# A two-block transformer on one core: copies, norms and gate tiles reordered around the weight splits, output in four pieces

## The chip, the cores and the metric

The kernel is one launch on one core of a Trainium2 chip. The metric is the device time of that launch in microseconds, from the chip's profiler. Engines are named PE (TensorE; PEld is its weight load), DVE (VectorE), ACT (ScalarE), POOL (GpSimd) and SP (SyncE, which issues DMAs). Each engine runs its own instructions in program order; between engines there are semaphores.

## The reference

All is fp32. The activations are x, 1 x 256 x 1024; two memories of 256 x 1024 are attended to. Cut to its shape:

```python
def first_block(x, mem, ...):                       # DEPTH = 2
    for layer in range(DEPTH):
        mix = even_mixer(x, ...) if layer % 2 == 0 else odd_mixer(x, ...)
        x = layer_norm(DEEPNORM_ALPHA * x + mix, ...)
        x = layer_norm(DEEPNORM_ALPHA * x + memory_cross_attention(x, mem, ...), ...)
        x = layer_norm(DEEPNORM_ALPHA * x + swiglu(x, ...), ...)

def second_block(x, mem, ...):
    for l in range(DEPTH):
        x = layer_norm_2(DN_ALPHA * x + 0.5 * swiglu_ffn(x, ffn_w_in[l, 0], ffn_w_out[l, 0]), ...)
        x = layer_norm_2(DN_ALPHA * x + mixer_sublayer(x, ...), ...)
        x = layer_norm_2(DN_ALPHA * x + memory_cross_attention_2(x, mem, ...), ...)
        x = layer_norm_2(DN_ALPHA * x + 0.5 * swiglu_ffn(x, ffn_w_in[l, 1], ffn_w_out[l, 1]), ...)
```

The even mixer is four heads of a two-directional mLSTM (a chunked scan with decays and a running maximum) beside eight heads of neighbourhood attention. The odd mixer is differential attention with rotary positions and an RMS norm per head. `mixer_sublayer` adds three branches, each behind a sigmoid gate and a projection: attention over a latent of width 128 restricted to the 64 best keys of each query, stick-breaking attention, and a short causal convolution.

## The kernel before

**Stages.** `SUB` lists 14 stages, j = 0 to 13: even, cross, ffn, odd, cross, ffn, then twice ffn, merge, cross, ffn. "Merge" is `mixer_sublayer`. A cross of the first block has four heads of 256 and is called long here; one of the second block has four heads of 128 and is called single. The whole program is written out instruction by instruction for each engine; there is no loop on the chip.

**Products and weights.** Every fp32 product is three matmuls (helper at L354): high part of the one by high part of the other, and the two mixed ones. So every operand is split into a high and a low half. A weight tile is 128 x 2048 elements, 1 MB. SyncE transfers it into a ring of RAW = 3 buffers, ScalarE copies the high half out (`wh`, L1226), VectorE subtracts to get the low half (`wl`, L1754). The raw buffer is free for another transfer when both have read it. The split tiles stand in a ring of PARTS = 3. The first tiles of a stage ("entry tiles") have places of their own, named front, side, back, mem, note and under. The activations of a stage are transposed by TensorE and copied out of PSUM as `xh` (ScalarE, L1257) and `xl` (VectorE); attention outputs likewise as `oh` and `ol` (L1788, L2201).

**What sets the order.** `get(name, look)` on ScalarE and VectorE is "wait for the PSUM bank `name`"; ahead of that wait it makes the split of every weight tile that TensorE will use up to `look` tiles beyond the bank's own (PARTS − 1 by default; None makes none, `ahead(name, look)` only splits). A copy or a norm written behind such a call therefore stands behind the split, 1.8 us on ScalarE and 2.2 us on VectorE. `take` hands TensorE its PSUM banks in turn, `free` gives one back when it has been copied, `await_read` waits for that.

**Even stage** (TensorE L772 on, ScalarE L1420 on, VectorE L1997 on). VectorE copies `av` (L2055) out of two banks after the wait for Silu and a scaling of the keys (L2050); the decay maxima follow (L2066), then on ScalarE the copies `cn` (L1482). In the neighbourhood attention TensorE per unit does scores, products of the output projection, head outputs, and the transpose of the probabilities.

**Cross stages.** `softmax` (ScalarE L1317 on, VectorE L1884 on) goes through the heads: maxima, exponentials, normalisation (L1916), and `after(t)`, the copies of head outputs. `out_proj` (L510 on) does the output projection in steps (half of x, four k parts); with kc = 4 (single cross) its first step may start with a part of the input ready ("gradual"). It also places the entry tiles of the next stage. VectorE then adds the residual (L1844), norms and stores x (L1868), one half of 512 columns after the other. In a single cross VectorE copies `xv` (L1937) and makes the low parts `ol` before it.

**Odd stage.** `enter` (L560 on) runs the first projections over the entry tiles. In the attention loop VectorE does maxima, a rotary step `rope(t + 2)` and the probabilities of the unit before (L2156 on).

**Merge.** The last loop (TensorE L1136 on) has steps t = −1 to 11. Step t does the transposes of unit t − 2, the scores of unit t, for odd t the next two query products (`ql`, copied by ScalarE L1710), the latent products of unit t − 3, and for t ≥ 0 half a gate tile (a gate is `x` by a 1024 x 256 slice, ScalarE makes the sigmoid `gs`, L1613). `LATENT_GATES` says at which step ScalarE reads a finished gate. Then come four column groups n of three branch products each, with the last four gate tiles between them, and `merged` parts (L2420 on).

**Output.** SyncE waits for the last x and stores all of it by one DMA (L2618 to L2620).

## Time and profile before

| | before |
|---|---|
| median of 3 runs | 2274.41 us (2272.13 to 2275.5) |
| the profiled execution | 2275.15 us |
| its span in the trace | 2273.4 us |
| PE busy | 2218.6 us, 98% |
| PEld busy | 2055.5 us, 90% |
| DVE busy | 1436.1 us, 63% |
| ACT busy | 1063.6 us, 47% |
| POOL busy | 103.5 us, 5% |
| mean DMA rate | 181 GB/s |

The time of an execution is that of the device, the span runs from the first to the last instruction in the trace; 1.75 us lie outside it. "Busy" counts the time in which an engine works on an instruction. PE at 98% leaves 54.8 us in which it does nothing. In the 40 slices of the page PE stands at 9 (90% or more) in all but the last, where it is 8, and so does PEclk, the clock that the throttle granted. By stages, from the timeline: even from 14 to 162 us, long crosses to 282 and at 576 to 705, odd 465 to 576, merges about 1080 to 1290 and 1781 to 1983, single crosses 1340 to 1396 and 2042 to 2088. The last matmul ends at 2263.9, the last x at 2268.9 us.

### The profile page before, as it was taken

The page shows a single profiled execution, that of the slowest core. Times are in us where ns is not written, and L with a number is a line of the kernel's source. Part 1 is how long each engine was busy: PE and PEld are TensorE (multiplying, and loading weights), DVE is VectorE, ACT ScalarE, POOL GpSimd, SP SyncE. Part 2 cuts the span into 40 slices and gives each one's busy share as a digit, 9 for nine tenths or more (in the row PEclk, how much of TensorE's full clock was granted, in tenths as well). Part 3 has the DMA queues.
Part 4 walks back from the last instruction along what each step waited for, and adds up shares of the span by engine and source line. Part 5 has one row for each costly group of instructions (what it writes and reads, how often), then busy time and mean ns, then how long its engine had stood idle before and what let it go on. Part 6 is the DMA issues. An engine that isn't in the chain of part 4 may idle for free.

```text
span 2273.4 us, 38286 instructions
## 1 busy us (share of the span) xinstructions
PE 2218.6 (98%) x16065; PEld 2055.5 (90%) x16065; DVE 1436.1 (63%) x1679; ACT 1063.6 (47%) x1289; POOL 103.5 (5%) x174
## 2 busy tenths in 40 slices
PE   9999999999999999999999999999999999999998
PEld 9879899888889999998998998998998998998996
DVE  6776655567756556565765676556555866677554
ACT  4554444446454443443556454443443555454442
POOL 2310000000000000000011000000000002000000
PEclk9999999999999999999999999999999999999999
DMA  7656465653645665566643664666566553565553
GB/s 245 190 158 223 142 193 186 222 154 119 204 149 168 198 218 176 191 209 194 190 140 96 213 223 156 196 200 207 180 195 198 180 164 113 187 229 161 186 180 117
DMA packets 348219, 411.90 MB, mean 181 GB/s; under 512 B 11404, under 2 KB 280904, under 8 KB 347920
## 3 DMA queue, kind: packets, MB, share of 16 engines
q1 hardware_dynamic: 338880, 377.19, 51.7%
q0 software_dynamic: 9168, 32.26, 4.6%
q8 instruction: 129, 2.11, 0.4%
q14 instruction: 42, 0.34, 0.0%
HBM read 406.51 MB, written 5.00 MB: 181 GB/s over the span
## 4 chain that ended last, share of the span: by engine, by line
PE 86%; DVE 6%; ACT 4%; issue 3%; DMA 1%; DVEq 0%; SPq 0%; ACTq 0%
PE bank L354 86%; ACT wh L1226 1%; DVE wl L1754 1%; DMA raw<-in_even_w_in 1%; ACT prob L1704 1%; DVE nmax L2382 0%; DVE qkT L2030 0%; DVE logit L2379 0%; PE bank L1192 0%; DVE en_l L1754 0%; ACT en_h L1226 0%; DVE x L1868 0%; DVE z L1863 0%; DVE nmax L1906 0%; DVE stat L1829 0%
## 5 line engine op out<-in xcount | busy, mean ns | idle before, releaser
L1754 DVE TENSOR_TENSOR wl<-raw,wh 128x2048 fp32r<-128x2048 f32 (+1 forms) x352 | 762.5, 2172 | 528.3 <-ACT wh L1226 445.0
L354 PE MATMUL bank<-xl,wh 128*128 128x256 f32 x3144 | 877.7, 279 | 7.2 <-issue 3.0
L354 PE MATMUL bank<-xh,wl 128*128 128x256 f32 x3144 | 870.7, 277 | 0.0
L354 PE MATMUL bank<-xh,wh 128*128 128x256 f32 x3144 | 870.7, 277 | 0.0
L1226 ACT ACTIVATE wh<-raw 128x2048 fp32r<-128x2048 f32 (+1 forms) x352 | 637.6, 1817 | 316.5 <-PE bank L354 295.0
L354 PEld LDWEIGHTS bank<-xl,wh 128*128 128x128 f32 x3144 | 591.0, 188 | 15.3 <-issue 12.1
L354 PEld LDWEIGHTS bank<-xh,wl 128*128 128x128 f32 x3144 | 589.7, 188 | 0.8 <-issue 0.2
L354 PEld LDWEIGHTS bank<-xh,wh 128*128 128x128 f32 x3144 | 590.2, 188 | 0.2
L354 PE MATMUL bank<-wl,hh 128*128 128x512 f32 x528 | 205.9, 390 | 0.0
L354 PE MATMUL bank<-wh,hh 128*128 128x512 f32 x528 | 205.5, 389 | 0.0
L354 PE MATMUL bank<-wh,hl 128*128 128x512 f32 x528 | 205.5, 389 | 0.0
L354 PEld LDWEIGHTS bank<-wh,hh 128*128 128x128 f32 x528 | 99.1, 188 | 20.6
L354 PEld LDWEIGHTS bank<-wh,hl 128*128 128x128 f32 x528 | 99.1, 188 | 20.4
L354 PEld LDWEIGHTS bank<-wl,hh 128*128 128x128 f32 x528 | 99.1, 188 | 20.2
L1403 ACT ACTIVATE gate_s<-bank 128x512 f32<-128x512 f32 x54 | 32.4, 600 | 180.7 <-PE bank L354 180.7
L354 PE MATMUL bank<-wl,oh 128*128 128x512 f32 x224 | 90.2, 403 | 10.0 <-DVE ol L1788 3.9
L354 PE MATMUL bank<-wh,oh 128*128 128x512 f32 x224 | 88.2, 394 | 0.0
L354 PE MATMUL bank<-wh,ol 128*128 128x512 f32 x224 | 87.9, 392 | 0.0
L2457 POOL DMA_DIRECT2D gb<-in_ln_g x14 | 7.6, 540 | 1378.2 <-DVE x L1868 1374.6
L1257 ACT ACTIVATE xh<-bank 128x512 fp32r<-128x512 f32 x56 | 30.3, 600 | 77.0 <-PE bank L354 77.0
L1284 ACT ACTIVATE mv<-mv 128x1 f32<-128x1 f32 x28 | 5.7, 203 | 122.5 <-DVE mv L1855 122.4
L354 PEld LDWEIGHTS bank<-wl,oh 128*128 128x128 f32 x224 | 42.4, 189 | 20.6 <-issue 9.6
(385 smaller groups left out, 3118.8 us busy)
## 6 DMA issues: line engine op xcount, KB each, us to landing
raw<-in_ffn_w_in SPq DMA_DIRECT2D x80, 1024.0 KB, 5.2
raw<-in_w_mix_in SPq DMA_DIRECT2D x56, 1024.0 KB, 5.3
raw<-in_ffn_w_gu SPq DMA_DIRECT2D x40, 1024.0 KB, 5.2
raw<-in_ffn_w_out SPq DMA_DIRECT2D x40, 1024.0 KB, 5.1
raw<-in_ffn_w_down SPq DMA_DIRECT2D x20, 1024.0 KB, 5.0
raw<-in_mem_wkv SPq DMA_DIRECT2D x16, 1024.0 KB, 5.5
raw<-in_even_w_in SPq DMA_DIRECT2D x13, 1024.0 KB, 6.9
raw<-in_w_branch SPq DMA_DIRECT2D x24, 512.0 KB, 3.4
```

Source lines behind the costliest of these rows:

```text
L354: ins = pe.transpose(o, a, b) if transpose else pe.matmul(o, a, b, start=start, stop=stop)
L1226: act.activation(part_of(t, 0), raw_tile(t), ACT.Copy).then_inc(sig("w_high"), 1)
L1257: act.activation(dst, src, ACT.Copy).then_inc(sig("part_high"), 1)
L1284: act.activation(mv[:, t, 2:3], mv[:, t, 1:2], ACT.Sqrt).then_inc(sig("std_ready"), 1)
L1403: free(("gate", j, q), act.activation(gate_s[:, q % 2, :], o[:, :], ACT.Silu))
L1704: ins = act.activation(prob[:, g % 2, keys_of[tb]], logit[:, g % 2, keys_of[tb]], ACT.Exp, bias=nmax[:, g % 2, tb:tb + 1], accum_out=psum_ ...
L1754: dve.tensor_tensor(part_of(t, 1), raw_tile(t), part_of(t, 0).bitcast(F32), ALU.subtract)\
L2457: pool.dma_start(gb[:, i, :], v.partition_broadcast(P)).then_inc(sig("gains_loaded"), 16)
```

## The change

- **Even:** VectorE copies `av` before the wait for Silu and without splitting ahead; both engines split for "cum" up to PARTS tiles beyond. ScalarE's copy of the table goes ahead of Silu, `query(0)` ahead of the second exponentials, and a one-column exponential is added before `query(1)`. In TensorE's loop the transposes of the probabilities stand ahead of the products of the output projection, and one step of that projection is spread over two units.
- **Long cross:** the first projection step waits for its input two parts at a time, in place of one wait for all; the normalisation stands ahead of `after`, which is one unit later; the last ring tile is ordered ahead of the entry tile.
- **Entry to odd:** one of the eight products of the second tile is done after the transposes of x instead of before them.
- **Odd:** on VectorE `rope(t + 2)` stands behind the probabilities; ScalarE's `late_values(0)` is a step earlier; two transposes of normed heads stand ahead of the second half of a projection; VectorE looks ahead at ("dw", 1, 1).
- **Merge:** gate halves are done one step earlier from step −1 on, by `HALF_GATES`; two branch products fill steps 10 and 11; both engines split one tile further at n = 1, VectorE before the low part of `merged`.
- **Single cross:** the copies of `xv` and `oh` don't split ahead; the entry splits of the two engines move: ScalarE's first behind `oh`, VectorE's first to where its second stood, the second behind the first x.
- **Output:** four DMAs of 256 KB, each after its quarter of x.

```diff
@@ -281,7 +281,8 @@
 FILLERS = (("conv", 0), ("conv", 1), ("conv", 2), ("gate", 0), ("conv", 3), ("conv", 4), ("conv", 5), ("gate", 1))
-LATENT_GATES = {1: 2, 3: 3, 5: 4, 7: 5, 9: 6, 11: 7}
+LATENT_GATES = {0: 2, 1: 3, 3: 4, 5: 5, 7: 6, 9: 7}
+HALF_GATES = {-1: (0,), 0: (1, 2), **{t: (t + 2,) for t in range(1, 10)}}
 BRANCHES = (1, 2, 0)
@@ -530,7 +531,7 @@
                     entry_tiles[j + 1] = tiles
-            elif early and (i or kc != HC) and kc != 4:
+            elif early and (i or kc != HC) and kc != 4 and not (i and kc == KC):
                 tiles.append(order_entry(j + 1, turns[len(tiles)], early.pop(0)))
@@ -597,12 +598,14 @@
                         take(name, "acc")
-                    block_products(name, 0, tile, t, 4 * m, 4, m == 0, m == 1, m == 1)
+                    cut = 3 if t == 0 and m == 1 and len(tiles) == 2 else 4
+                    block_products(name, 0, tile, t, 4 * m, cut, m == 0, cut == 4 and m == 1, cut == 4 and m == 1)
+                    if cut == 3:
+                        x_to_T(i, [1])
+                        block_products(name, 0, [part[:, 3:4, :] for part in tile], t, 7, 1, False, True, True)
                 else:
...
                     block_products(("ckv", layer, t), 0, tile, t, 0, KC, True, True, True)
-            if t == 0 and len(tiles) == 2:
-                x_to_T(i, [1])
         for slot in ("front", "side"):
@@ -732,8 +735,11 @@
             if c == 2 and t == 5:
-                await_parts(base + 2)
-                y_step(j, wo, *steps[0], 4 * c, oh, ol)
+                half, k0 = steps[0]
+                tile = y_tile(j, wo, half, k0, 4 * c)
+                y_products(j, 0, half, k0, 4 * c, oh, ol, tile, need=lambda k: await_parts(base + 1 + (k - 1) // c))
+                y_products(j, 1, half, k0, 4 * c, oh, ol, tile)
+                owed[0] += 1
             if t >= 3:
@@ -923,14 +929,6 @@
                 score(t + 1)
-            if t < 4:
-                await_parts(mlstm_parts)
-                y_step(j, wo, t - 2, 0, KC, oh, ol)
-            if t == 5:
-                held = [y_tile(j, wo, half, 4, KC) for half in range(2)]
-            if t in (5, 7):
-                await_parts(mlstm_parts + (t - 3) // 2)
-                second_half(4 + (t - 5) // 2)
             if t >= 4 and t % 2 == 0:
@@ -939,9 +937,19 @@
                 transposed_probs(u, lambda tb, kb: prob[:, u % 2, tb * S + kb * P:tb * S + kb * P + P])
-            if t == 9:
-                await_parts(mlstm_parts + 3)
-                second_half(6)
+            if t == 2:
+                await_parts(mlstm_parts)
+                y_step(j, wo, 0, 0, KC, oh, ol)
+            if t == 3:
+                late = y_tile(j, wo, 1, 0, KC)
+            if t in (3, 4):
+                y_products(j, t - 3, 1, 0, KC, oh, ol, late)
+                owed[0] += t - 3
+            if t == 5:
+                held = [y_tile(j, wo, half, 4, KC) for half in range(2)]
+            if t in (5, 7, 9):
+                await_parts(mlstm_parts + (t - 3) // 2)
+                second_half(4 + (t - 5) // 2)
         unit[0] += 8
@@ -1052,9 +1060,11 @@
         head_out(7, "work")
+        normed_to_T(4)
+        normed_to_T(5)
         first_half(1)
-        for u in range(4, 8):
-            normed_to_T(u)
+        normed_to_T(6)
+        normed_to_T(7)
         mem_to_T(j + 1)
@@ -1130,6 +1140,10 @@
         stick_parts = len(halves)
+        def branch_tile(n, i):
+            proj_T(("branch", l_, n, i), [A["w_branch_2"][l_, i][:, n * S:n * S + S]], 4, yh, yl, k0=4 * i)
         for t in range(-1, 8 + 4):
@@ -1164,17 +1178,21 @@
                        ("lat", l_, u) if kb == 1 else None)
-            if t >= 0:
-                gate = half_gate(l_, 2 + t // 2, t % 2, gate if t % 2 else None)
+            for half in HALF_GATES.get(t, ()):
+                gate = half_gate(l_, 2 + half // 2, half % 2, gate if half % 2 else None)
+            if t >= 10:
+                await_parts(stick_parts)
+                branch_tile(0, BRANCHES[t - 10])
         unit[0] += 8
...
                     gate_tile(l_, 3 * n + pos)
-                if n == 0:
-                    await_parts(base if i == 0 else stick_parts)
-                proj_T(("branch", l_, n, i), [A["w_branch_2"][l_, i][:, n * S:n * S + S]], 4, yh, yl, k0=4 * i)
+                if n == 0 and i == 0:
+                    await_parts(base)
+                if n or i == 0:
+                    branch_tile(n, i)
             parts(("merged", l_, n), in_bank=False)
@@ -1353,11 +1371,11 @@
             free(name, act.activation((probT, bm)[u // 2][:, u % 2, :], o[:, :], ACT.Copy))
-        split_to(entry_tiles[j + 1][0])
         for u in range(4):
             name = ("O", unit[0] + u)
-            o = get(name)
+            o = get(name, None)
             high(name, oh[:, u, :], o[:, 0:S])
+        split_to(entry_tiles[j + 1][0])
         unit[0] += 4
@@ -1448,11 +1466,11 @@
         ahead(("aqk", 3), PARTS)
-        ahead("cum")
+        ahead("cum", PARTS)
+        o = get("tab")
+        free("tab", act.activation(btab[:, :], o[0:8, :], ACT.Copy))
         wait("conv_done", 1)
         act.activation(qkT[:, :, :], qkT[:, :, :], ACT.Silu).then_inc(sig("silu_done"), 1)
-        o = get("tab")
-        free("tab", act.activation(btab[:, :], o[0:8, :], ACT.Copy))
@@ -1471,8 +1489,8 @@
                 gate(1)
+                query(0)
                 ahead(("kN", 1))
-        query(0)
         ahead(("bq", 0))
@@ -1491,6 +1509,7 @@
         act.activation(ao[:, :, :], ao[:, :, :], ACT.Sigmoid).then_inc(sig("ao_ready"), 1)
+        act.activation(gT[:, 0:1], gT[:, 0:1], ACT.Exp, scale=0.0)
         ahead(("bq", 1))
@@ -1563,8 +1582,6 @@
                 probs_T(unit[0] + t - 2)
-            if t == 7:
-                late_values(0)
             g = unit[0] + t
@@ -1572,6 +1589,8 @@
                 rope_tile(t + 3)
+            if t == 6:
+                late_values(0)
             if 3 <= t < 7:
@@ -1723,7 +1742,7 @@
                     gate_tile(l_, 3 * n + pos)
-            ahead(("branch", l_, n, BRANCHES[2]))
+            ahead(("branch", l_, n, BRANCHES[2]), PARTS if n == 1 else PARTS - 1)
             wait("merged_ready", 4 * l_ + n + 1)
@@ -1822,7 +1841,7 @@
             if half and j + 1 in entry_tiles:
-                split_to(entry_tiles[j + 1][1 if single and t == 0 else -1])
+                split_to(entry_tiles[j + 1][0 if single and t == 0 else -1])
             o = get(name, 0 if single or t and (half or by_block) and not cross_after(j) else PARTS - 1)
@@ -1869,6 +1888,8 @@
                 x_to_T(j + 1, [t])
+            if single and t == 0:
+                split_to(entry_tiles[j + 1][1])
         if cross_after(j):
@@ -1890,8 +1911,12 @@
                 neg_max(unit[0] + t, biased)
-            if t >= 3:
+            if biased and t >= 3:
                 after(t - 3)
+            if not biased and t >= 4:
+                after(t - 4)
+        if not biased:
+            after(n_units - 1)
         unit[0] += n_units
@@ -1933,13 +1958,13 @@
             name = ("xv", j, t, 0)
-            o = get(name)
+            o = get(name, None)
             free(name, dve.tensor_copy(xv[:, t, 0:512], o[:, :]))
...
             low(name, ol[:, u, :], o[:, 0:S], oh[:, u, :])
-        split_to(entry_tiles[j + 1][1])
+        split_to(entry_tiles[j + 1][0])
         unit[0] += 4
@@ -2045,14 +2070,14 @@
            .then_inc(sig("decay_cols"), 1)
-        ahead(("av", 1))
+        for t in range(TB):
+            name = ("av", t)
+            o = get(name, None)
+            free(name, dve.tensor_copy(av[:, t, :, 0:P], quad(o[:, :])))
+        ahead("cum", PARTS)
         wait("silu_done", 1)
...
            .then_inc(sig("qk_ready"), 1)
-        for t in range(TB):
-            name = ("av", t)
-            o = get(name)
-            free(name, dve.tensor_copy(av[:, t, :, 0:P], quad(o[:, :])))
         wait("decay_cols", 1)
@@ -2211,8 +2236,6 @@
                 ins.then_inc(sig("neg_max"), 1)
-            if t + 2 < 8:
-                rope(t + 2)
             if 1 <= t <= 8:
@@ -2229,7 +2252,10 @@
                 ins.then_inc(sig("prob_ready"), 1)
+            if t + 2 < 8:
+                rope(t + 2)
         normed_heads(0, 4)
+        ahead(("dw", 1, 1), 1)
         for u in (4, 5):
@@ -2418,6 +2444,8 @@
                         ins.then_inc(sig("merged_ready"), 1)
+            if n == 1:
+                ahead(("branch", l_, n, BRANCHES[2]), PARTS)
             k = slice(2 * n, 2 * n + 2)
@@ -2615,9 +2643,12 @@
             c0 = c1
-    sp.wait_ge(sig("x_ready"), 4 * LAST)
-    sp.dma_start(out[0].rearrange("(t p) d -> p t d", p=P), x[:, :, :]).then_inc(out_stored, 16)
-    sp.wait_ge(out_stored, 16)
+    for t in range(TB):
+        for half in range(2):
+            f = slice(half * 512, half * 512 + 512)
+            sp.wait_ge(sig("x_ready"), 4 * (LAST - 1) + 2 * t + half + 1)
+            sp.dma_start(out[0, t * P:t * P + P, f], x[:, t, f]).then_inc(out_stored, 16)
+    sp.wait_ge(out_stored, 16 * 2 * TB)
```

## Rows read from the trace of the kernel before

**Rows 1.** Page: busy time and share of engines, and the costliest group of splits.
```profile
PE 2218.6 (98%) x16065; PEld 2055.5 (90%) x16065; DVE 1436.1 (63%) x1679; ACT 1063.6 (47%) x1289; POOL 103.5 (5%) x174
...
L1754 DVE TENSOR_TENSOR wl<-raw,wh 128x2048 fp32r<-128x2048 f32 (+1 forms) x352 | 762.5, 2172 | 528.3 <-ACT wh L1226 445.0
```
**Rows 2.** Waits of TensorE: waiting line, releaser, total us, count, mean us.
```profile
PE bank L354 <- ACT ql L1710: 4.9, 6, 1.4
...
PE bank L354 <- ACT gs L1613: 1.3, 4, 0.4
```
**Rows 3.** Timeline, 56 to 67 us: start, length, instruction, [idle before, releaser].
```profile
63.39 1.28 DVE L2055 COPY av<-bank 128x512 f32<-128x512 f32 x2
...
64.13 1.06 PE L354 MATMUL bank<-ident,cc_ 128*128 128x128 f32 x7 [4.02 <-DVE av L2055]
...
66.79 0.68 DVE L2066 TENSOR_REDUCE mm_<-bank 128x4 f32<-128x512 f32 x1
```
**Rows 4.** Windows: stretch, its length, busy PE/PEld/DVE/ACT/POOL, PEclk, DMA share, GB/s.
```profile
65.10:68.40 3.30, 3.30 (x17) 3.30 (x17) 3.27 (x4) 0.00 (x0) 3.30 (x7) 0.50 1.02 375
1382.00:1386.00 4.00, 1.83 (x12) 1.24 (x11) 3.67 (x6) 0.97 (x3) 0.00 (x0) 1.00 0.56 177
1386.00:1389.40 3.40, 3.40 (x11) 2.63 (x10) 2.80 (x4) 0.43 (x1) 0.00 (x0) 0.50 0.02 7
...
2078.20:2081.60 3.40, 3.40 (x23) 3.06 (x22) 2.75 (x4) 0.48 (x1) 0.00 (x0) 1.00 0.00 0
```
**Rows 5.** Timeline, 85 to 87 us: the copy of cn and its first reader.
```profile
85.52 0.38 ACT L1482 ACTIVATE cn<-bank 128x260 f32<-128x260 f32 x1
...
86.04 0.36 PE L354 MATMUL bank<-xl,wh 128*128 128x256 f32 x1 [1.45 <-ACT cn L1482]
```
**Rows 6.** Timeline, 143 to 149 us, softmax of the even stage.
```profile
143.09 2.29 DVE L1754 TENSOR_TENSOR wl<-raw,wh 128x2048 fp32r<-128x2048 f32 x1 [0.23 <-ACT wh L1226]
...
148.59 0.47 PE L354 MATMUL bank<-wl,oh 128*128 128x512 f32 x1 [1.58 <-DVE ol L1788]
```
**Rows 7.** Timeline, 245 to 263 us, first long cross attention.
```profile
245.53 0.66 PE L354 MATMUL bank<-ident,prob 128*128 128x128 f32 x4 [0.56 <-DVE prob L1916]
...
262.85 0.47 PE L354 MATMUL bank<-wl,oh 128*128 128x512 f32 x1 [1.69 <-DVE wl L1754]
```
**Rows 8.** Timeline at the entry to the odd stage and before its output projection.
```profile
465.77 0.47 PE L354 MATMUL bank<-front_l,xh 128*128 128x512 f32 x1 [1.69 <-ACT xh L1257]
...
561.11 0.47 PE L354 MATMUL bank<-wl,oh 128*128 128x512 f32 x1 [2.09 <-DVE ol L2201]
```
**Rows 9.** Timeline, 1191 to 1202 us, latent loop of the first merge.
```profile
1191.70 0.47 PE L354 MATMUL bank<-xl,wh 128*128 128x256 f32 x1
...
1194.72 0.82 PE L354 MATMUL bank<-ckT,ql 128*128 128x128 f32 x4
...
1196.21 2.29 DVE L1754 TENSOR_TENSOR wl<-raw,wh 128x2048 fp32r<-128x2048 f32 x1 [1.11 <-issue]
...
1200.95 0.71 PE L354 MATMUL bank<-ckT,ql 128*128 128x128 f32 x3 [1.44 <-ACT ql L1710]
```
**Rows 10.** Timeline, 1267 to 1271 us, last gate tile but one of that merge.
```profile
1267.93 2.29 DVE L1754 TENSOR_TENSOR wl<-raw,wh 128x2048 fp32r<-128x2048 f32 x1 [1.18 <-ACT wh L1226]
...
1270.33 0.35 PE L354 MATMUL bank<-xl,wh 128*128 128x256 f32 x1 [1.50 <-issue]
```
**Rows 11.** Timeline, 1369 to 1396 us, end of the first single cross attention.
```profile
1369.74 0.46 PE L354 MATMUL bank<-probT,xv 128*128 128x256 f32 x1 [1.53 <-DVE xv L1937]
...
1374.30 2.28 DVE L1754 TENSOR_TENSOR em_l<-raw,em_h 128x2048 fp32r<-128x2048 f32 x1
...
1394.97 0.75 DVE L1868 SCALAR_TENSOR_TENSOR x<-z,mv,gb 128x512 f32<-128x512 f32 x1
```
**Rows 12.** Page, DMA issues: transfer, queue, count, KB each, us to landing.
```profile
out<-x SPq DMA_DIRECT2D x1, 1024.0 KB, 4.0
...
ident<-in_consts SPq DMA_DIRECT2D x1, 64.0 KB, 2.0
```

## The prediction

> **What bounds the kernel now.** The page comes first: TensorE is busy for 2218.6 of 2273.4 us [rows 1]. The change removes no product, so all it can win is TensorE's idle time, 54.8 us, and the tail behind the last product. The list of TensorE's waits by releaser came second; it names many short ones, such as the query copies of both merges, 4.9 us in all [rows 2]. Third, the timeline around each wait, with VectorE (which makes the low half of every weight tile, 2.17 us each [rows 1]) and ScalarE (the high half) beside it: both run in program order, so a copy that stands behind a split is late by the split. For each wait the reader should ask whether the chain behind it gets shorter, or is only met at another place. Last, the granted clock by stretches, because a wait can cost more than its length: behind the 4.02 us wait of the first stage TensorE worked at 0.50 of its clock, the 1.2 GHz level, through 65.1 to 68.4 us [rows 3, 4].
>
> **The change, part by part.** "Gain" is against the profiled execution.
>
> First stage, decays. The bank that the decay products want is emptied by two copies of av, which stand behind a split and a wait for Silu [rows 3]. Moved ahead of both, they run at 57.1, so TensorE's 4.02 us go, and with them the slow clock behind it. But the next wait hangs on VectorE and ScalarE. VectorE now does copies (1.28), split (2.29), scaling (0.69), split (2.28) from 57.05 and starts the decay maxima at about 63.5 instead of 66.79, 3.3 earlier; the copies of cn on ScalarE [rows 5] come earlier by the same. Query copy and second exponentials only change places. So the products at 86.04 [rows 5] start at about 82.8, where the row's wait of 1.45 becomes an idle time of nearly 4, as TensorE is there at 79. That is as long as the wait behind which the clock fell; I charge half of one slow stretch, and somewhat more for its place: 3.2 − 1.3 = 1.9 gained, between 1.2 and 3.2. The 4.02 us is thus mostly not won.
>
> First stage, softmax. Transposes move ahead of output products, so that these cover the copies; the two waits of 1.58 and the one of 0.75 (at 140.9, 148.6 and 156.0; one stands for them [rows 6]) should go. But in the new order the third transpose no longer looks as far ahead in the weight ring: ScalarE splits the first cross tile only after the sixth unit's exponentials, and VectorE's split, at 143.09 to 145.4 now [rows 6], ends about 0.8 later while TensorE wants the sixth probabilities 3 earlier. I find an idle time of 3.4 before the sixth transpose and a gain of 1.4 behind it, of which a slow clock takes most. Gain 0.3, between 1.4 and −0.3. The exponential table fetched early (1.28 on ScalarE) is beside TensorE's work; it is part of that 1.4.
>
> Two long crosses. The normalisation goes ahead of the low parts, the first projection starts with two of four parts, and the last weight tile is split ahead of the entry tile. Waits: 0.56 before the transpose, about 0.3 behind it, 1.69 for the tile [rows 7], 2.6 each, with refilling of the pipeline about 3.1. VectorE has the same splits ahead of the layer norm, so TensorE meets x about 1.4 too early at the next transposes. 3.1 − 1.5 = 1.6 each, 3.2 in all, between 1.5 and 4.6.
>
> Odd entry and attention. One of eight products of the second tile (three matmuls of 0.23, 0.68 us) covers the xh/xl copies: 0.7 of the 1.69 wait [rows 8]. Inside attention probabilities go ahead of the rotary step on VectorE; but from the fifth unit on VectorE's total is what sets the pace and stays the same, so the wait met at one transpose is met at the next. The added look-ahead at ("dw",1,1) names a tile that is split already: it costs and gives nothing, and the split ahead of the ol copies, 2.09 us of wait [rows 8], stays. Gain 0.7, between −0.5 and 4.
>
> Two merges. Each loop step now has a half gate tile (1191.7 to 1194.7, about 2.9 us [rows 9]) between the query copy and its use. The waits for ql (4.9) and for gates (1.3) are 3.1 a merge [rows 2], 4.0 with refilling. Tiles are now ordered a step sooner, so VectorE's split comes ahead of the score addition at steps 0, 1 and 3 and no longer behind it; at 1196.21 it already holds up one such step, and 1.44 of wait follow [rows 9]. In the first steps I find 0.7 and 0.6 of this again, and some 0.3 of small ones: 2.4 gained. The two branch tiles in steps 10 and 11 are only moved, and cover the last copies. Then the gate tile at 1270.33 waits 1.50 for a split that stands behind the second merged parts [rows 10]; moved ahead, it starts at the landing, about 1.0 earlier. 3.4 each, 6.7 in all, between 3 and 10.
>
> Two single crosses. The xv copies go ahead of a split, so the 1.53 wait goes [rows 11]. From there VectorE is the bound: em, en and front splits, four layer norm halves, four low parts, back to back from 1374.30 to 1395.7 [rows 11]. The change has em start at 1373.9 at best (ScalarE makes its high half behind the four copies of O) and drops no piece, so the last x is ready at 1395.4: 0.3 gained. What was idle in three places (1.53, then 4.0 − 1.83 = 2.17 in the stretch 1382 to 1386 [rows 4]) gathers before the second transposes of x, over 4 us. In the first single cross the clock already fell to 0.50 behind the 2.17 [rows 4], where it was hidden; in the new place the ffn's products follow it, and up to 1.7 each is lost. I take 1.2 − 0.3 = 0.9 lost each, 1.8 in all, between +0.6 gained and 3.4 lost.
>
> Output. One DMA of 1024 KB lands 4.0 us after issue; 64 KB took 2.0 [rows 12]. Three of four pieces of 256 KB are gone before the last x; the last takes some 2.5. SyncE has nothing queued behind. Gain 1.5, between 0 and 2.0. The Trainium skill (DMA: Bandwidth & Descriptors, Anatomy of one DMA) gives a fixed 2.0 us and 436 KB a us beyond, as an estimate 2.6 for the last piece against 4.4 for all, a gain of 1.8; the two rows agree with it within 0.4. It also speaks against four pieces where they follow each other; here only the last is waited for.
>
> **Sum.** 1.9 + 0.3 + 3.2 + 0.7 + 6.7 − 1.8 + 1.5 = 12.5 us. 2275.15 − 12.5 = 2262.65 for a profiled execution, and 2274.41 − 12.5 = 2261.9 for the median (the profiled one was 0.7 above it). With all good ends, 3.2 + 1.4 + 4.6 + 4 + 10 + 0.6 + 2 = 25.8, 2248.6; with all bad ones 1.2 − 0.3 + 1.5 − 0.5 + 3 − 3.4 + 0 = 1.5, 2272.9.
>
> **Rivals.** One: VectorE has more slack in the single crosses than I gave it, and their waits go. For it: each wait there has one named releaser. Against: no gap over 0.8 us on VectorE in those 21 us. It would win 2 × (1.53 + 2.17 + 0.5) = 8.4 instead of losing 1.8: 2251.7.
> Two, the clock: each longer idle time (decays, softmax, single crosses) brings two slow stretches, not one. A stretch of 3.3 at 0.50 costs 1.65; at four places, and with the whole of the first two, 8 more: 2269.9. For it: [rows 4] shows one fall behind 4.02 and one behind 2.17. Against: behind the same waits of the second single cross the clock stays at 1.00 [rows 4]. The Trainium skill (TensorE: Matmul & The Clock Gate, What's actually happening) has the lower clock as the resting state, released by activity; the trace agrees, and by that rule gathering idle time in one place speaks against this change.
> Three: waits only move. The merges keep theirs, as the copies in the new first steps are as late as before; left are the crosses, the entry and the output, less the single crosses: 3.2 + 0.7 + 1.5 − 1.8 = 3.6, 2270.8.
> Four, slower: the splits ahead of the score addition in the merges. Place: VectorE, six splits of 2.29 in each of two merges. As long as score, exponential and query copy together end within a half tile and the steps beside it, nothing is lost; from the point where the split starts later than the score is ready by more than this cover, each costs up to its length: 12 × 2.29 = 27.5, against 5.8 won elsewhere, 2296; at half of that 2282.
> Five: it does not do what it says. The look-ahead at ("dw",1,1) and the early table fetch are such edits; they carry nothing in the sum.
>
> **Chances.** Forecast 0.66, one 0.12, two 0.07, three 0.10, four 0.05. The 80% range: 2250 to 2269.5, from below rival one to almost rival two, and it takes in most of the bounds. 0.2% is 4.5 us, about what a measurement of this kernel tells from no change. Faster: forecast, one, half of two, a fifth of three: 0.84. Same: the rest of two and three, 0.11. Slower: 0.05.
>
> **What would show it.** Right: no wait for av; a wait near 4 us on cn; waits for ql halved; the wait on xv gone and a long one on x before the second transposes, with 0.50 of clock behind it; ol L2201 still near 2. Wrong: if the idle time in the single crosses vanishes, VectorE did not bind; if ql waits grow beyond 4.9, the splits in the merges bind; if the clock is at 1.00 all through, the 5 us charged for it come on top.

## The result and the profile after

| | before | after |
|---|---|---|
| median | 2274.95 us (4 runs, 2272.13 to 2276.0) | 2262.05 us (4 runs, 2261.33 to 2262.74) |
| ratio to before | | 0.9948, 95% interval 0.9937 to 0.996 |
| span of the profiled execution | 2273.4 us | 2259.5 us |
| last matmul ends | 2263.9 us | 2252.1 us |

The changed kernel is 12.9 us faster (12.4 against the first three runs of before); 12.5 was forecast. The traces differ by 13.8 us before rounding: 11.8 up to the end of the last matmul and 2.0 behind it. Line numbers below are those of the changed kernel or of the experiment; they are up to some 40 higher than before. The page's busy rows and its group of splits, for [rows 1]:

```profile
PE 2215.7 (98%) x16065; PEld 2053.5 (91%) x16065; DVE 1437.0 (64%) x1679; ACT 1064.1 (47%) x1290; POOL 105.7 (5%) x174
...
L1773 DVE TENSOR_TENSOR wl<-raw,wh 128x2048 fp32r<-128x2048 f32 (+1 forms) x352 | 763.0, 2172 | 523.3 <-ACT wh L1244 443.1
```

The work is the same, 16065 matmuls; what fell is idle time. The waits of TensorE by releaser (total us, count, longest; the third number of [rows 2] is the longest too, not a mean), for [rows 2, 3, 5, 7, 8, 11]:

```profile
PE bank L355 <- DVE x L1887: 12.8, 12, 3.2
...
PE bank L355 <- DVE prob L1941: 3.0, 1, 3.0
PE bank L355 <- ACT cn L1500: 2.9, 1, 2.9
PE bank L355 <- DVE ol L2226: 2.3, 2, 2.1
PE bank L355 <- ACT ql L1729: 2.1, 4, 0.5
...
PE bank L355 <- ACT ao L1477: 1.1, 1, 1.1
```

The wait on av is gone, one of 1.1 on ScalarE's copy `ao`, 5 us ahead of cn, is new, the one on cn has grown from 1.45 to 2.9, ql has fallen from 4.9 to 2.1, gs from 1.3 to nothing, ol L2226 stays, and the wait on x has grown. Its places, and the ones of cn and of the softmax, in the timeline (start, length, instruction, idle before and releaser):

```profile
81.97 0.36 PE L355 MATMUL bank<-xl,wh 128*128 128x256 f32 x1 [2.85 <-ACT cn L1500]
...
143.89 0.66 PE L355 MATMUL bank<-ident,prob 128*128 128x128 f32 x4 [2.99 <-DVE prob L1941]
...
555.00 0.76 PE L355 MATMUL bank<-wl,oh 128*128 128x512 f32 x1 [2.08 <-DVE ol L2226]
...
1363.87 2.29 DVE L1773 TENSOR_TENSOR em_l<-raw,em_h 128x2048 fp32r<-128x2048 f32 x1 [1.37 <-ACT em_h L1244]
...
1384.11 0.62 PE L355 MATMUL bank<-ident,x 128*128 128x128 f32 x3 [3.16 <-DVE x L1887]
1384.55 0.75 DVE L1887 SCALAR_TENSOR_TENSOR x<-z,mv,gb 128x512 f32<-128x512 f32 x1
```

Windows of the changed kernel (length, busy PE, PEld, DVE, ACT, POOL, granted clock, DMA share, GB/s), for [rows 4]:

```profile
145.40:148.70 3.30, 3.30 (x9) 2.20 (x7) 1.70 (x5) 1.09 (x4) 0.00 (x0) 0.50 0.30 103
555.00:558.30 3.30, 3.30 (x8) 2.62 (x9) 1.52 (x5) 1.52 (x1) 0.00 (x0) 0.50 0.74 239
1384.40:1387.70 3.30, 2.89 (x15) 2.49 (x13) 2.05 (x4) 1.79 (x3) 1.05 (x2) 0.50 0.42 142
1266.00:1291.00 25.00, 25.00 (x223) 25.00 (x222) 16.62 (x13) 11.65 (x13) 0.00 (x0) 1.00 0.75 244
```

The clock fell behind the waits of 3.0, 2.1 and 3.2 us (and at 2073.9, behind the same wait in the second single cross), not behind the one of 2.9 at cn. Before, it fell at two places. The last row is about a matter of its own, below.

Where the time went, by stage. Each line takes one matmul that both programs have at the end of the stage, its start in either trace, and the change of the difference since the line above:

| up to | before | after | difference | of this stage | forecast |
|---|---|---|---|---|---|
| first transpose | 9.3 | 8.6 | 0.8 | 0.8, start-up | |
| decays | 124.2 | 119.9 | 4.3 | 3.5 | 1.9 |
| even softmax | 156.0 | 152.1 | 4.0 | -0.3 | 0.3 |
| first long cross | 454.5 | 449.1 | 5.4 | 1.5 | 1.6 |
| odd | 600.1 | 595.2 | 4.9 | -0.6 | 0.7 |
| second long cross | 877.3 | 871.3 | 6.0 | 1.2 | 1.6 |
| first merge | 1335.1 | 1325.0 | 10.1 | 4.0 (0.1 of it ffn) | 3.4 |
| first single cross | 1569.5 | 1560.2 | 9.3 | -0.8 | -0.9 |
| ffn | 1752.5 | 1742.9 | 9.6 | 0.2 | |
| second merge | 2031.5 | 2018.7 | 12.8 | 3.3 | 3.4 |
| second single cross, last matmul | 2263.9 | 2252.1 | 11.8 | -1.0 | -0.9 |
| output | 2273.4 | 2259.5 | 13.8 | 2.0 | 1.5 |

A pair of traces is one execution of each kernel. The experiments below run most stages again in one order or the other, so the same stretches (between matched matmuls) can be averaged over up to 14 traces. By these means, start-up and ffn aside, the change wins 1.8 in the decays (2 traces with the order of before, 9 with the new one), −0.3 in the even softmax (4 and 10), 1.4 and 1.3 in the long crosses (2 and 12), 0.2 in odd (1 and 10), 2.8 and 2.7 in the merges (2 and 12), −1.4 and −1.5 in the single crosses (3 and 8). With the output that is 9.0 us.

### The profile page after: what moved, and what is told of

It is laid out like the page before. It is cut to its first block, busy times and chain, and to the rows that moved or that the text cites. A ratio compares the mean times of both kernels' runs of the same rounds, so it can differ in the third digit from the quotient of the medians.

```text
span 2259.5 us, 38296 instructions
## 1 busy us (share of the span) xinstructions
PE 2215.7 (98%) x16065; PEld 2053.5 (91%) x16065; DVE 1437.0 (64%) x1679; ACT 1064.1 (47%) x1290; POOL 105.7 (5%) x174
## 4 chain that ended last, share of the span: by engine, by line
PE 87%; DVE 6%; issue 3%; ACT 3%; DMA 0%; DVEq 0%; ACTq 0%; SPq 0%
PE bank L355 87%; ACT wh L1244 1%; DVE wl L1773 1%; DVE qkT L2055 1%; DMA raw<-in_w_mix_in 0%; DVE x L1887 0%; DVE z L1882 0%; DVE stat L1848 0%; DVE front_l L1773 0%; DVE z L1846 0%; PE bank L1210 0%; ACT prob L1723 0%; DVE nmax L2408 0%; DVE en_l L1773 0%; DVE em_l L1773 0%
## 5 line engine op out<-in xcount | busy, mean ns | idle before, releaser
L1846 DVE SCALAR_TENSOR_TENSOR z<-x,bank 128x512 f32<-128x512 f32 x56 | 38.3, 684 | 31.5 <-PE bank L355 31.0
```

The costliest lines, as they stand in the source:

```text
L1846: free(name, dve.scalar_tensor_tensor(z[:, t, f], x[:, t, f], ALPHA / c, o[:, :], ALU.mult, ALU.add))
```

## The experiments

All but the last two are the changed kernel with one edit. "At 200 us" and the like are starts of matched matmuls in the traces, start-up taken off. Executions of one kernel scatter by several us, and the traces show three things that differ from one to the next (the clock, the pace of the matmuls, and when an early weight tile lands, all below), so a part of 1 or 2 us is read from the trace and the median only bounds it.

### The output in one DMA: no_out

The four DMAs replaced by the one of before.

> The changed kernel (2262.05) with its output stored by one DMA again, all else as changed. Theory (only the last quarter of the output is waited for): slower by the 2.1 us by which the stretch behind the last matmul got shorter (9.46 before, 7.37 after, in the two traces), so 2264.1; the prediction had 1.5. Rival (the shorter end of the trace lies in the records, not in the time): no change, 2262.0. Everything ahead of the output is instruction for instruction the same, so this trace also tells what repeats from one execution to the next: theory, the waits come back within 0.1 us each, while the four stretches at 0.50 of the clock (145.3, 554.9, 1384.4, 2073.9 us) and the stretches in which a matmul of 128x256 takes 117.8 instead of 113.4 ns may move; rival, those come back at the same places too and so belong to the order of the program.

Measured: 2267.5 us (2262.7 to 2271.0), ratio 0.9965 (0.9951 to 0.9978). The stretch behind the last matmul is 2266.9 − 2257.5 = 9.4 us, against 7.4: 2.0 us, as expected. The DMA view gives the reason; the last 256 KB land as fast as 64 KB did [rows 12] (count, KB each, us to landing; changed kernel):

```profile
out<-x SPq DMA_DIRECT2D x4, 256.0 KB, 2.0
```

The other 3 us of the median are not the output's. Ahead of it the program is the changed one, and yet the trace is 6.3 us late at 200 us. Of this, 2.2 us were lost before the clock fell, at the wait on `ao`, which was 1.09 in the changed kernel's trace: VectorE began the copies of av at 57.05 here and at 55.52 there. That goes back to the landing of a weight tile, which ScalarE's split awaits, first in the changed kernel, then in this one:

```profile
30.95 1.92 ACT L1244 ACTIVATE wh<-raw 128x2048 fp32r<-128x2048 f32 x1 [2.46 <-DMA raw<-in_even_w_in]
```

```profile
32.50 1.92 ACT L1244 ACTIVATE wh<-raw 128x2048 fp32r<-128x2048 f32 x1 [4.67 <-DMA raw<-in_even_w_in]
```

The two waits in the decays of this kernel:

```profile
78.84 3.19 PE L355 MATMUL bank<-av,pk 128*128 128x130 f32 x16 [3.51 <-ACT ao L1477]
...
83.73 0.55 PE L355 MATMUL bank<-xl,wh 128*128 128x256 f32 x1 [1.70 <-ACT cn L1500]
```

The window from the clock's fall at 79.5, which lies between them:

```profile
79.50:89.70 10.20, 8.50 (x41) 8.23 (x40) 8.24 (x7) 6.70 (x13) 0.00 (x0) 0.50 0.61 187
```

Here it stayed at 0.50 for 10.2 us, which made the stretch up to 100 us 2.9 longer, and for 6.8 at 147.8, in place of 3.4, which cost 1.2 more; in the changed kernel's trace it did not fall in the decays at all. So a wait offers the fall, and an execution takes it or not. The Trainium skill (TensorE: Matmul & The Clock Gate, What's actually happening) has the clock low by default and released by activity. The direction agrees here, 0.50 behind a wait of 3.5 us; whether a given wait is enough is not the program's alone: the same wait of 2.1 us (`odd_look` below) had a fall behind it in 6 of 11 traces.

### The single crosses as before: no_single

```diff
@@ ScalarE, single_cross
+            split_to(entry_tiles[j + 1][0])
             for u in range(4):
-                o = get(name, None)
+                o = get(name)
                 high(name, oh[:, u, :], o[:, 0:S])
-            split_to(entry_tiles[j + 1][0])
@@ VectorE, residual and single_cross
-                    split_to(entry_tiles[j + 1][0 if single and t == 0 else -1])
+                    split_to(entry_tiles[j + 1][1 if single and t == 0 else -1])
...
-                o = get(name, None)
+                o = get(name)
                 free(name, dve.tensor_copy(xv[:, t, 0:512], o[:, :]))
```

> The changed kernel with the order of before in the two single cross attentions alone (xv behind a split, first entry split early, second ahead of the first x). Theory (VectorE binds from the first entry split to the last x, 21.4 us in either trace, so the change only gathered idle time in one place and called up the slow clock): faster by 0.9 each, 2260.2. Rival one (the early first x and the waits on xv were worth what they lasted): slower by 2 x 1.7 to 2 x 3.9, 2265.5 to 2270. Rival two (the clock falls by chance, not by the length of the wait): the same as the changed kernel within 0.6.

Measured: 2258.68 us (four of five runs 2258.3 to 2258.8), ratio 0.9933 (0.9921 to 0.9946): 3.4 faster than the changed kernel by the medians, with intervals that overlap. By the trace 0.8 and 0.7 come from the two single crosses, and 1.5 from the clock, which happened not to fall at 555 us. What settles it are the table's two stages, from the end of the merge to a matmul of the ffn behind the cross, over all traces: with the order of before 234.4 to 234.9 us and, in the second, 232.1 to 232.4 (three traces), with the changed order 235.2 to 237.1 and 233.1 to 234.3 (eight traces). The two groups don't touch. TensorE's waits are those of before again:

```profile
1358.77 1.97 PE L355 MATMUL bank<-probT,xv 128*128 128x256 f32 x8 [1.53 <-DVE xv L1960]
1372.72 0.66 PE L355 MATMUL bank<-ident,x 128*128 128x128 f32 x4 [1.40 <-DVE x L1887]
1374.17 0.66 PE L355 MATMUL bank<-ident,x 128*128 128x128 f32 x4 [0.80 <-DVE x L1887]
1383.57 0.63 PE L355 MATMUL bank<-ident,x 128*128 128x128 f32 x4 [0.97 <-DVE x L1887]
```

VectorE goes from the start of em's split (1363.33) to the end of the last x (1384.76) in 21.43 us; in the changed kernel 1363.87 to 1385.30, 21.43; before, 1374.30 to 1395.72, 21.42. It is the same chain in all three, so rival one of this run falls. Rival two falls by counting. With the wait of 3.2 us the clock fell in 16 of 16 single crosses (eight traces with the changed order), with the waits spread out (1.4 and 0.8 behind each other) in 3 of 6 (before, this kernel, and `best` below). And there a fall costs little, as VectorE sets the pace: the first single cross took 234.4 us in before, with a fall, and 234.4 in this kernel, without one.

### Another order of the entry: single_gu

```diff
+            if SUB[i - 1][:2] == ("cross", 2):
+                for t in range(TB):
+                    if t:
+                        x_to_T(i, [1])
+                    await_parts()
+                    take(("gu", i, t), "acc", frees=2)
+                    for m in range(2):
+                        block_products(("gu", i, t), m * S, arrived(tiles[m]), t, 0, KC, True, True, m > 0)
+                for t in range(TB):
+                    take(("gv", i, t), "acc", frees=2)
+                    block_products(("gv", i, t), 0, arrived(tiles[2]), t, 0, KC, True, True, True)
...
-                if single and t == 0:
-                    split_to(entry_tiles[j + 1][1])
+                if single:
+                    split_to(entry_tiles[j + 1][1 + t])
```

> The changed kernel, where behind the two single crosses the feed-forward entry runs in another order: em and en for the first 128 rows, em and en for the second, then front for both; VectorE splits front behind the second x instead of ahead of it. In the changed kernel VectorE is busy back to back from the first entry split to the last x (21.4 us) and TensorE waits 3.16 us for the second x, and the clock falls behind it. Theory (VectorE binds; only what stands ahead of the last x counts): the second x comes 2.3 us earlier, the wait shrinks to about 0.9, the split of front (2.29) is covered by em and en of the second rows, and the clock stays: 2 x 2.3 to 2 x 3.9, 2254.2 to 2257.5. Rival one (the front split is only moved and TensorE meets it at the front products): 2262.0. Rival two (the clock falls at the shorter wait as well): 2257.5.

Measured: 2261.97 us (2257.95 to 2266.97), ratio 0.9952 (0.9939 to 0.9965). The theory's number was wrong. The second x did come 2.2 earlier, but the products of the second rows need the copies of that x, which front's products had covered:

```profile
1383.12 0.66 PE L355 MATMUL bank<-ident,x 128*128 128x128 f32 x4 [0.76 <-DVE x L1901]
1384.57 0.66 PE L355 MATMUL bank<-ident,x 128*128 128x128 f32 x4 [0.80 <-DVE x L1901]
1386.75 0.36 PE L355 MATMUL bank<-em_l,xh 128*128 128x256 f32 x1 [1.53 <-ACT xh L1289]
```

Three waits of 3.1 us together for the 3.16 and 0.4 before: 0.5 won each, and the clock fell in one of two places instead of both (1.1 won there). Moving a VectorE piece within the stretch wins next to nothing; that was the forecast's reading, and here I had forgotten it.

### Part of VectorE's work on GpSimd: pool_en

```diff
+                pool.wait_ge(sig("w_low"), n)
+                pool.tensor_tensor(part_of(n, 1), raw_tile(n), part_of(n, 0).bitcast(F32), ALU.subtract)\
+                    .then_inc(sig("w_low"), 1)
...
                 if single and t == 0:
-                    split_to(entry_tiles[j + 1][1])
+                    split_to(entry_tiles[j + 1][2])
```

> The changed kernel, where in each of the two single crosses the low half of the entry tile en (128x2048) is made by GpSimd instead of VectorE, and VectorE splits front at the place where it split en. Theory (VectorE binds from the first entry split to the last x: moving work within it, as the kernel with the other entry order did, won only 0.46 us each, taking 2.29 us off it must win them): the last x comes 2.3 us earlier, the wait of 3.16 for it shrinks to about 0.9, and the transposes' copies stay covered by the products with front. GpSimd's multiplications of 128x256 take 0.75 us each, so 2048 columns 6 us as an estimate, 1366.1 to 1372, ahead of its first reader at 1378: 2 x 2.3, and up to 1.6 of slow clock each: 2254.3 to 2257.5. Rival one (GpSimd and VectorE slow each other, or GpSimd needs more than 12 us): VectorE's ops beside it lengthen and the gain is gone, 2261 to 2268. Rival two (ScalarE or TensorE sets the end of this stretch as soon as VectorE is relieved): under 1 us each, 2260 to 2262.

Measured: 2261.69 us (2258.57 to 2264.17), ratio 0.9936 (0.9923 to 0.9949). The median is that of the changed kernel; by the trace 1.4 and 1.6 are won in the two places, with the clock down in both, behind waits of 2.1 and 0.8. Neither the theory's 2.3 nor rival two; rival one has the mechanism (the two engines slow each other) but not its size, as part of the gain is left. GpSimd and VectorE, from the timeline:

```profile
1370.57 4.59 POOL L2513 TENSOR_TENSOR en_l<-raw,en_h 128x2048 fp32r<-128x2048 f32 x1 [37.50 <-DVE em_l L1777]
1371.02 0.69 DVE L1852 BATCH_NORM_STATS2 stat<-z 128x6 f32<-128x512 f32 x1
1371.75 0.69 DVE L1850 SCALAR_TENSOR_TENSOR z<-x,bank 128x512 f32<-128x512 f32 x1
...
1373.52 2.20 DVE L1886 SCALAR_TENSOR_TENSOR z<-z,mv,gb 128x512 f32<-128x512 f32 x1
```

Beside GpSimd's instruction the operations on a PSUM bank keep their 0.69 us; the first one that reads two SBUF operands (z and gb) takes 2.20 instead of 0.74 (its like took 0.75 before [rows 11]) and ends 0.56 behind GpSimd's, so 1.46 of the 2.29 saved are given back. The Trainium skill (GPSIMD Engine Reference, 1. Specifications) says that the two engines share their SBUF interfaces and contend when VectorE's instruction has two SBUF inputs; the trace agrees, in which operations it hits and which not.

### The two merges as before: no_merge

The edits to `LATENT_GATES`, `HALF_GATES`, the branch products in steps 10 and 11 and the look-ahead at n = 1, all undone.

> The changed kernel with the order of before in the two merges alone (gate halves a step later, branch products behind the loop, no look-ahead at the gate tile). Theory (waits for query copies and gates): the two traces give 3.95 and 3.26 us, 7.2 in all, of which about 2.5 is not waits but a matmul pace of 113.4 instead of 117.8 ns; so 2269.3 if that pace goes back with the order, 2266.7 if it doesn't. The prediction had 6.7: 2268.8. Rival (waits only move, what came in was luck in pace): 2262.0 to 2264.5.

Measured: 2268.23 us (8 runs, 2264.66 to 2271.96), ratio 0.9973 (0.9963 to 0.9983): 6.2 slower than the changed kernel; by the trace 2.7 and 3.3, 6.0. About 1.2 of the 3.3 is the pace told of below. The waits return to within a tenth (the view of waits of this kernel):

```profile
PE bank L354 <- ACT ql L1720: 4.9, 6, 1.4
...
PE bank L354 <- ACT gs L1623: 1.4, 4, 0.4
```

So the rival (luck) falls. But one part of what the first two traces show between 1267 and 1304 us is luck. The same matmuls run at two paces, 113.4 and 117.8 ns from start to start, at clock 1.00 both: before, 215 of them began in 25 us, against 223 in the window of the changed kernel shown above.

```profile
1275.00:1300.00 25.00, 25.00 (x215) 25.00 (x214) 15.00 (x13) 11.63 (x13) 0.00 (x0) 1.00 0.70 225
```

The slower pace holds from one wait to a later one and costs 285 x 4.4 ns = 1.3 us in the gate and branch section of a merge. With the new order it stood there in 7 of 24 sections (12 traces), with the old in 3 of 4, this kernel having it in its second merge and not in its first. So it is not bound to the order; whether the order shifts the odds, four sections don't say.

### The decays as before: no_decay

av behind a split and Silu, the copies of the table and of the first query late.

> The changed kernel with the order of before around the decays alone (av behind a split and Silu, table copy and first query copy late). Theory, from the two traces up to 124 us: the change won 3.1 us there (4.0 at the wait on av, 0.6 of slow clock, 1.3 given back at the wait on cn), so undoing it costs 3.1: 2265.2; the wait on av comes back with 4.0 and the one on cn falls from 2.9 to 1.5. The prediction had 1.9: 2264.0. Rival (the longer wait on cn calls up the slow clock in about half of the executions, 1.6 to 5.9 us each, and eats the gain): 2262 to 2263.

Measured: 2267.54 us (2263.85 to 2268.69), ratio 0.9969 (0.9957 to 0.9981). In the trace the wait on av is back, 3.63 us, the one on cn is short, and at the matmul behind cn the kernel is 2.9 us later than the changed one. The theory stands for this pair of traces. But the changed kernel's trace is the best of the nine with this order, up to 100 us: they took 87.2 to 92.3 us from the first transpose on, 88.7 on average, against 90.7 in before and 90.3 here, so the mean gain is 1.8. Two things make the spread. The wait on `ao` was 1.1 to 3.7 us, 2.2 on average; it goes with the landing told of under `no_out`: ScalarE began that split 22.4 us behind the first transpose in the changed kernel's trace, 24.4 in `no_out` and 24.9 in `no_single`, with waits on ao of 1.1, 3.5 and 3.7. And the clock fell in four of the nine, in three of them before the wait on cn began; they lost 2.9, 1.6, 0.2 and nothing, 0.5 on average, since the wait on cn behind it hides a part. So the rival is half right: chance eats part of the gain, but mostly at `ao`, and not all of it.

### cn ahead of the split: cn_first

```diff
-            ahead(("bq", 0))
             for d in range(2):
                 for half in range(2):
                     name = ("KV", d, half)
-                    o = get(name)
+                    o = get(name, None)
```

> The changed kernel with the copies of cn on ScalarE no longer behind the split for bq (1.9 us, 79.66 to 81.55): they don't split ahead. Theory: TensorE's wait at 81.97 (2.85 us) ends when ScalarE is through the second exponentials, at 79.7, so it shrinks by 1.8, and the split behind it has slack, since its low half is wanted only at 89: 2260.2, and less in executions in which the clock fell behind that wait (79.5 us in the kernel with one output DMA, 10.2 us at 0.50, 5.9 us lost). Rival (the split is wanted as soon as the copies: its low half stands behind the decay products on VectorE): the wait moves to the next weight tile, 2262.0.

Measured: 2261.68 us (2256.39 to 2263.71), ratio 0.9944 (0.9932 to 0.9956). ScalarE and TensorE there:

```profile
77.87 2.03 PE L355 MATMUL bank<-av,pk 128*128 128x130 f32 x16 [1.80 <-ACT ao L1477]
78.11 2.44 ACT L1487 ACTIVATE cm<-cm,mm_ 128x128 f32<-128x128 f32 x8
80.45 1.19 ACT L1499 ACTIVATE cn<-bank 128x260 f32<-128x260 f32 x4
80.96 0.36 PE L355 MATMUL bank<-xl,wh 128*128 128x256 f32 x1 [1.06 <-ACT cn L1499]
```

The wait on cn fell by 1.8 (2.85 to 1.06), as expected, but the one on ao ahead of it is 0.7 longer in this trace (1.80 against 1.09). That is within what it does in kernels without the edit (1.1 to 3.7). Behind it, from 82.5 to 100 us of before, this kernel, `best` and `best_pool4` took 16.6 to 16.8 us, and the five others with the changed order and no fall of the clock 18.4 to 18.6: the edit is worth 1.6. In the profiled execution the longer wait on ao and a second stretch of slow clock at 142 us hid it.

### The long crosses as before: no_long

> The changed kernel with the order of before in the two long crosses alone (all four parts awaited at once, the normalisation behind the low parts, the entry tile ahead of the last weight tile). Theory: each cross loses the three waits again (0.56 and 0.3 at the transpose, 1.69 at the weight tile, 2.6 with refilling) and gets back what the earlier x now waits (0.76 and 0.96 at the transposes of x): by the two traces 1.46 and 1.17, so 2264.7. The prediction had 3.2: 2265.2. Rival (VectorE sets the pace up to the last x here too, as in the single crosses): no change, 2262.0.

Measured: 2265.91 us (2265.18 to 2268.46), ratio 0.9967 (0.9955 to 0.9979). By the trace 1.4 and 1.2, the theory's numbers; the median's 3.9 holds more than that. The rival (VectorE binds here too) falls: ahead of the first x the reordering wins 3.2 us, then 1.8 go back at x and its copies.

### One tile further at dw: odd_look

```diff
-            ahead(("dw", 1, 1), 1)
+            ahead(("dw", 1, 1), PARTS - 1)
```

> The changed kernel with one number changed: the look-ahead at (dw, 1, 1) on VectorE reaches two tiles instead of one. By the trace one tile further is the split at 552.17 that holds up the ol copies (2.08 us of wait at 555.0), while VectorE is idle from 548.8 to 550.1. Theory: the split goes into that idle time, ends at about 550.9, the ol copies start at about 552.7 and TensorE's wait shrinks from 2.08 to about 0.4; and with a shorter wait the clock, which fell at 554.9, stays: 1.6 to 3.3 us faster, 2258.8 to 2260.4. Rival one: the split delays the scaling of heads 4 and 5 by as much as it no longer delays ol, and the wait moves ahead of the transposes: no change. Rival two: the clock falls all the same: 2260.4.

Measured: 2261.61 us (2258.03 to 2263.1), ratio 0.994 (0.9927 to 0.9952). The split sits in VectorE's idle time and the wait is what was expected:

```profile
548.34 2.28 DVE L1773 TENSOR_TENSOR wl<-raw,wh 128x2048 fp32r<-128x2048 f32 x1
...
553.05 0.47 PE L355 MATMUL bank<-wl,oh 128*128 128x512 f32 x1 [0.55 <-ACT oh L1567]
```

3.1 us won through the odd stage: 1.5 of wait and 1.5 because the clock did not fall. With the wait of 2.1 us it fell in 6 of 11 traces (before among the five without), with 0.55 in none of three. The median shows only 0.4 of it; this execution ran both single crosses with the clock down (three stretches) and much at the slow pace.

### The even softmax as before: no_evensoft

> The changed kernel with the order of before in the softmax of the even stage alone (output products ahead of the transposes of the probabilities, no early exponential). In the changed kernel TensorE waits 3.0 us there at one place, and behind it the clock fell to 0.50 in six of the nine traces so far (one or two stretches of 3.4 us, 1.6 us lost for each); before, the same idle time lay in five waits of 0.3 to 1.75. Theory (the reordering wins 1.4 in waits and loses 1.6 in two executions of three): the waits of 1.58 come back, no slow clock there, the trace at 200 us within 0.6 of an undisturbed one of the changed kernel plus 1.4; time 2262.0 plus or minus 1. Rival one (the spread-out waits call up the slow clock as well): 2263.4. Rival two (the waits gained more than that, the clock fell by chance elsewhere): 2263.4 to 2265.

Measured: 2264.5 us (2260.6 to 2269.89), ratio 0.9955 (0.9942 to 0.9968). In the trace the five waits are back (4.8 us together, against 4.1 in two), and the clock doesn't fall behind them; it fell in none of four traces with this order and in 7 of 10 with the new one, 11 stretches of 3.4 us. From 100 to 156 us of before the four took 55.9 to 56.0 us; with the new order it was 54.7 without a fall (three traces), 56.3 with one stretch (three), 57.5 with two (four). So the reordering wins 1.2 where the clock stays and loses 0.3 on average. The median points the other way, 2.4 slower: the profiled execution had seven slow stretches elsewhere. By the traces this part of the change is worth next to nothing.

### The pieces together: best, and best_pool4

`best`: odd_look and cn_first put in, single crosses and even softmax in the order of before.

> The changed kernel with the two gains found put in (look-ahead of two tiles at dw, cn copied ahead of the split) and the two parts that gather idle time taken out (single crosses and softmax of the even stage in the order of before). Theory (waits add up, and where the idle time is spread out the clock falls less often): by the traces 1.5 at the ol wait, 1.1 at the cn wait, 0.75 in each single cross, and in the softmax 0.85 more waits against on average 1.1 slow stretches of 1.6 less: 1.5 + 1.1 + 1.5 + 0.9 = 5.0, and one stretch less at 555 us in two executions of three, 1.0: 2256.0, between 2254.5 and 2258. Rival one (the clock falls as often, at other waits): 2258 to 2260. Rival two (parts don't add, each only moves the wait for the next): 2261 to 2262.

Measured: 2257.09 us (2256.09 to 2257.87), ratio 0.9924 (0.991 to 0.9937): 5.0 faster than the changed kernel. By the trace it is 4.0: 1.6 in the decays, 0.3 in the softmax, 3.5 in odd and 1.3 in the single crosses, less 2.9 in the merges, where the slow pace and a fall of the clock happened to stand. The theory's range held. Its reason, fewer falls of the clock, is argued and not shown: the trace has two slow stretches, the others 2 to 8, but `no_single` and `single_gu` have two as well; and while its five runs lie within 1.8 us and those of the experiments above within 3 to 9, the changed kernel's four, with the long waits, lie within 1.4.

`best_pool4`: as `best`, but the single crosses in the new order with en on GpSimd in four pieces.

```diff
+                for c in range(0, TILE, TILE // 4):
+                    f = slice(c, c + TILE // 4)
+                    ins = pool.tensor_tensor(part_of(n, 1)[:, f], raw_tile(n)[:, f],
+                                             part_of(n, 0)[:, f].bitcast(F32), ALU.subtract)
+                ins.then_inc(sig("w_low"), 1)
```

> The same, but in the single crosses the order of the change with the low half of en on GpSimd, in four pieces of 128x512 instead of one instruction of 128x2048. In the kernel with the one instruction (4.59 us on GpSimd) VectorE's z<-z,mv,gb beside it took 2.20 us instead of 0.74 and ended with GpSimd's, and the first x came 1.46 late. Theory (the operation of VectorE that reads two SBUF operands waits for the end of GpSimd's running instruction): with pieces of about 1.15 us it waits 1.15 at most, so z takes under 1.9 and x comes at least 0.3 earlier than with one piece; the last x comes 1.5 to 2.0 earlier than in the order of the change, against 0 to 0.3 for the kernel beside this one: 1 to 3 us faster than that one, 2253 to 2256, unless the clock falls behind the longer wait for the first x, 1.6 each. Rival (the pieces take turns with VectorE's operations, each of which then waits anew): VectorE's next three operations are each longer by 0.5 to 1.2, and nothing is won over one piece: 2256 to 2259.

Measured: 2254.11 us (2253.72 to 2254.72), ratio 0.9911 (0.9897 to 0.9924): 7.9 faster than the changed kernel, 3.0 faster than `best`. The time is the theory's, the mechanism is half the rival's:

```profile
1362.66 5.46 POOL L2511 TENSOR_TENSOR en_l<-raw,en_h 128x512 fp32r<-128x512 f32 x4 [37.49 <-DVE em_l L1773]
...
1365.61 1.40 DVE L1882 SCALAR_TENSOR_TENSOR z<-z,mv,gb 128x512 f32<-128x512 f32 x1
...
1367.24 1.43 DVE L1887 SCALAR_TENSOR_TENSOR x<-z,mv,gb 128x512 f32<-128x512 f32 x1
```

The pieces take turns: two operations of VectorE are 0.66 and 0.68 longer, 1.34 in all against 1.46 with one piece. So cutting won 0.1; what makes the kernel faster is en off VectorE, against the order of before: TensorE's waits in the two single crosses are 3.4 and 3.0 us in place of 4.4 and 5.3 in `best`, and each cross is 1.2 shorter. The rest of the 3.0 us isn't tied to this edit; in the traces a fall of the clock in `best`'s second merge, 1.8, stands against 1.0 in the decays. And it is faster although the clock fell in both of its single crosses, behind 2.0 and 0.8 us.

## Why the prediction was right, by its steps

**Decays, 1.9 forecast, 3.5 measured, 1.8 in the mean of the traces.** The mechanism was right in size: "an idle time of nearly 4" is there, as 1.09 on ao and 2.85 on cn, and the chain to cn came 3.5 earlier where 3.2 was forecast. Half of one slow stretch and more, 1.3, was charged for the new idle time, and none came in this execution. Over the nine traces about as much is lost, but mostly by a longer wait on ao (1.1 more than here on average) and only 0.5 by the clock.

**Even softmax, 0.3 and −0.3, the same in the mean.** Forecast 3.4 idle ahead of the sixth transpose, measured 2.99, with the slow clock behind it. The 1.4 won where the clock stays is 1.2, and the clock takes 1.6 or 2.8 of it in 7 of 10 traces.

**Long crosses, 3.2 and 2.6.** 3.1 forecast ahead of x and 1.5 given back; measured 3.2 and 1.8 in the first.

**Odd, 0.7 and −0.6.** The entry gave 0.7 (the difference goes from 5.4 to 6.1), the attention nothing, the look-ahead at ("dw", 1, 1) nothing, and the wait of 2.09 on ol stayed: all as written. What was missing is a term for the clock at that wait, 1.5 us: before, it did not fall there, and the forecast took this for a property of the place. In the four traces in which it didn't fall with the new order either, the stage gained 1.0; the mean of ten is 0.2.

**Merges, 6.7 and 7.2, and here a step failed.** The loop was to give 2.4 each and gave 2.3 and 2.4. The gate tile behind it was to "start at the landing, about 1.0 earlier" and gave 0.3 and −0.4: the split was freed, but the landing itself is now what ends last, as ScalarE's row shows.

```profile
1257.10 1.92 ACT L1244 ACTIVATE wh<-raw 128x2048 fp32r<-128x2048 f32 x1 [3.66 <-DMA raw<-in_w_mix_in]
...
1261.50 0.36 PE L355 MATMUL bank<-xl,wh 128*128 128x256 f32 x1 [1.18 <-issue]
```

The wait of 1.50 [rows 10] became 1.18 and, in the second merge, 1.89; over the twelve traces with this order it was 1.0 to 2.2. In place of the missing 2.1 us came 2 x 1.3 of the faster pace, which has nothing to do with the step. The waits' share is about 4.6, within the range given but 2 below the value taken; the mean of the traces, pace and clock included, is 5.5.

**Single crosses, −1.8 and −1.8.** The last x came 0.3 earlier, as forecast; the idle time gathered ahead of the second transposes (3.16 and 0.4, "over 4" was said) and the clock fell behind it, every time. This part makes the kernel slower, and undoing it helped. That the sizes agree is luck in part: the mean over the traces is 2.9 lost, not 1.8. The 2.17 us behind which the prediction saw the clock fall [rows 4] are two waits, 1.37 and 0.80.

**Output, 1.5 and 2.0.** Mis-sized: the last piece was taken at 2.5 us and lands in 2.0. The estimate of 2.6 that the prediction works out from the Trainium skill (DMA: Bandwidth & Descriptors, Anatomy of one DMA) is 0.6 too high as well; the fit there is for DMAs issued by GpSimd, these are SyncE's, and the measurement decides.

**The sum.** The total agreed to 0.2 us by the medians, closer than its parts: decays and output are 1.6 and 0.5 above, odd 1.3 and softmax 0.6 below, and the gate tiles' error is covered by the pace. Two single executions differ by 1 to 6 us in clock, pace and the wait on ao alone, so no agreement better than that was earned. The means of the parts add up to 9.0, not 12.5: 1.2 of the difference lies in the merges, 1.1 in the single crosses, 0.6 each in softmax, long crosses and odd. The mechanisms were right but for the gate tiles, and that 12.9 was met so closely was luck in good part.

**The rivals.** One (the single crosses win 8.4) is refuted by `no_single`. Two (the clock falls for two stretches, not one) is true of some executions: in 7 of the 16 single crosses with the changed order and in 4 of 10 in the softmax it stayed low for two, and `no_out`, the same program up to the output, was 6.3 us late at 200 us, 4.1 of it by the clock. As a median of the changed kernel it did not happen. Three (waits only move) is refuted by `no_merge`. Four (the splits ahead of the score addition bind) did not appear, the ql waits fell. Five is right for the look-ahead, which had been set one tile short.
